# Twenty-four transposes of the identity between the first transposes of x and the first weight unit

## The reference, cut to what matters

```
h = rms_norm(x, g_mix)          # x: 256 x 2048
proj = h @ w_in                 # the first columns computed are those of f
q, k, v, z, f, scal, gates = split(proj)
```

## Time and profile before

| | us |
|---|---|
| median of three runs | 2469.17 |
| the three runs | 2468.76, 2469.17, 2470.74 |
| profiled execution, its own time | 2468.13 |
| its span in the trace | 2466.3 |
| TensorE busy | 2437.7 (99%) |
| VectorE busy | 1534.6 (62%) |
| ScalarE busy | 1031.7 (42%) |
| mean DMA rate | 193 GB/s |

### The profile page before, as it was taken

One profiled execution on the slowest core, in us unless ns is written; L12 is line 12 of the kernel. 1 busy time (PEld: TensorE's weight loads), 2 busy tenths in 40 slices (PEclk: granted clock), 3 DMA queues, 4 the chain that ended last, 5 costly groups with the idle time before them and its releaser, 6 DMA issues.

```text
span 2466.3 us, 31871 instructions
## 1 busy us (share of the span) xinstructions
PE 2437.7 (99%) x13450; PEld 1995.1 (81%) x13450; DVE 1534.6 (62%) x1525; ACT 1031.7 (42%) x859; POOL 267.7 (11%) x222
## 2 busy tenths in 40 slices
PE   8999999999999999999999999999999999999997
PEld 7788888878888887887888888887777778888886
DVE  6465466557676445455445467789999965446664
ACT  4453345324334443433443434443434444544332
POOL 0002200210000000000000000045566400000000
PEclk9999999999999999999999999999999999999999
DMA  7343444346754555455555556675555576566653
GB/s 269 114 151 130 144 168 170 118 137 241 262 200 175 182 193 188 172 191 185 188 189 195 187 200 202 223 243 189 190 195 193 191 280 235 173 240 224 256 196 137
DMA packets 84094, 475.72 MB, mean 193 GB/s; under 512 B 8688, under 2 KB 8816, under 8 KB 32368
## 3 DMA queue, kind: packets, MB, share of 16 engines
q1 hardware_dynamic: 83952, 473.64, 54.8%
HBM read 450.54 MB, written 23.07 MB: 192 GB/s over the span
## 4 chain that ended last, share of the span: by engine, by line
PE 97%; DVE 1%; DMA 1%; issue 0%; ACT 0%; SPq 0%; DVEq 0%; ACTq 0%
PE acc L2071 30%; PE acc L2073 29%; PE acc L2072 29%; PE banks L2229 3%; PE banks L2082 2%; PE banks L2285 1%; PE banks L2352 1%; PE banks L2365 1%; PE banks L2182 1%; DMA av<-spilled 0%; PE banks L2405 0%; PE banks L2387 0%; PE banks L2203 0%; DMA c_in<-in_c_im 0%; DMA raw<-in_w 0%
## 5 line engine op out<-in xcount | busy, mean ns | idle before, releaser
L1257 DVE TENSOR_TENSOR w_lo<-raw,w_hi 128x2048 fp32r<-128x2048 f32 x394 | 908.2, 2308 | 560.6 <-ACT w_hi L815 559.6
L815 ACT ACTIVATE w_hi<-raw 128x2048 fp32r<-128x2048 f32 x394 | 751.7, 1914 | 600.7 <-DMA raw<-in_w 600.5
L2071 PE MATMUL acc<-w_hi,a_hi 128*128 128x512 f32 x2112 | 842.3, 399 | 9.5 <-DVE x_rows L1421 3.8
L2072 PE MATMUL acc<-w_lo,a_hi 128*128 128x512 f32 x2112 | 824.6, 390 | 0.0
L2073 PE MATMUL acc<-w_hi,a_lo 128*128 128x512 f32 x2112 | 824.4, 390 | 0.0
L2071 PEld LDWEIGHTS acc<-w_hi,a_hi 128*128 128x128 f32 x2112 | 397.2, 188 | 110.1 <-issue 21.8
L2073 PEld LDWEIGHTS acc<-w_hi,a_lo 128*128 128x128 f32 x2112 | 397.3, 188 | 85.0
L2072 PEld LDWEIGHTS acc<-w_lo,a_hi 128*128 128x128 f32 x2112 | 397.6, 188 | 79.8 <-issue 1.4
L2071 PE MATMUL acc<-w_hi,b_hi 128*128 128x512 f32 x928 | 364.2, 392 | 0.0
L2073 PE MATMUL acc<-w_hi,b_lo 128*128 128x512 f32 x928 | 361.5, 390 | 0.0
L2072 PE MATMUL acc<-w_lo,b_hi 128*128 128x512 f32 x928 | 361.2, 389 | 0.0
(11 more groups left out here) (349 smaller groups left out, 1636.2 us busy)
## 6 DMA issues: line engine op xcount, KB each, us to landing
raw<-in_w SPq DMA_DIRECT2D x395, 1024.0 KB, 4.9
spilled<-stage SPq DMA_DIRECT2D x72, 256.0 KB, 6.0
gate_in<-spilled SPq DMA_DIRECT2D x20, 512.0 KB, 5.9
x_rows<-in_x SPq DMA_DIRECT2D x4, 512.0 KB, 8.4
x_rows<-in_x SPq DMA_DIRECT2D x1, 2048.0 KB, 9.4
mem_rows<-in_mem SPq DMA_DIRECT2D x2, 1024.0 KB, 6.5
spilled<-stage_b SPq DMA_DIRECT2D x8, 256.0 KB, 5.9
out<-y_rows SPq DMA_DIRECT2D x4, 512.0 KB, 2.7
```

Source lines behind the costliest of these rows:

```text
L815: act.activation(w_hi[:, n % HIGH, :], raw[:, n % RAW, :], ACT.Copy)\
L1257: dve.tensor_tensor(w_lo[:, n % RAW, :], raw[:, n % RAW, :], w_hi[:, n % HIGH, :].bitcast(F32), ALU.subtract).then_inc(lo_split, 1)
L2071: pe.matmul(o, hi[:, tk], wh, start=first, stop=False)
L2072: pe.matmul(o, hi[:, tk], wl, start=False, stop=False)
```

## The change

A constant `WARM = 24` is added. On TensorE, behind `x_in(0)` and before the first unit, 24 transposes are issued. Operand and identity are both `ident`, and the four 128-column quarters of bank 3 are written in turn. They wait for nothing of their own, signal nothing, and nothing reads their result; the bank is overwritten by the transposes of x that use it first.

```
@@ -35,6 +35,7 @@
 HIGH = 4
 AHEAD = 2
 EARLY = 2
+WARM = 24
 EPS = 1e-6
@@ -2437,6 +2438,8 @@
             pe.wait_ge(loaded["small"], 16)
             x_in(0)
+            for q in range(WARM):
+                pe.transpose(bank(3)[:, q % 4 * P:(q % 4 + 1) * P], ident, ident)
 
             def slot_work(n):
                 unit(n, 0)
```

## The result

The changed kernel takes 2476.36 us (median of 12 runs, 2475.54 to 2479.7) against 2468.71 us before (12 runs, 2466.81 to 2470.94): 7.7 us slower, ratio 1.0033 with a 95% interval of 1.0025 to 1.0041. The forecast was 2468.4, with a range to 2471.0. The profiled execution of the changed kernel took 2478.95 us with a span of 2477.1.

A forecast was written before the change was run, and what follows sets the result against it. TensorE's instruction stream, 99% busy, was taken as the bound. Of 1.2 us won at the start 0.5 stay: 2468.7 on the median's scale, less 0.3 credited for clock timing, gives 2468.4 us, range 2467.0 to 2471.0.

The forecast's parts named there:

- The cost of the transposes and the clock: At TensorE's start: 24 transposes from 6.59 us raise the clock at 8.7 and end at 10.2; 1.2 us won by piece 1.
- the wait at 11.3: At TensorE's second matmul group: a new wait for the second quarter of `w_lo`, ready at about 11.4 us.
- The rival of cold transposes: At the start: transposes stay 0.214 us apart, first weight matmul at 11.7, loss of 0.7 to 1.5 us; chance 0.42.
- The cap at unit 6: At unit 6: the chain from unit 5's nearly fixed landing, with 0.47 us to spare, leaves 0.5 of 1.2 us won.
- the forecast's -0.5: At unit 6: the net gain expected to remain of the 1.2 us won at the start, between 0.4 and 1.2.
- Behind unit 6 TensorE is again the bound, nothing is given back and nothing grows: From unit 6 to the end: TensorE 99% busy, so the 0.5 us gain stays unchanged.
- The prediction's last sign of being wrong: Late in the span: a difference between the two traces behind 60 us would speak against the forecast; no size given.
- The rival of a start that runs out of instructions: At the start: TensorE uses up its instructions while DMA is full, waiting up to 3.6 us, time 2472.8; chance 0.04.

The follow-up runs named there:

- e2: The changed kernel, 24 transposes kept, with TensorE's loop pinned to slot 0 of a 256-instruction block: 2464.39 us (0.9978).
- e1: The kernel before, no transposes, with TensorE's loop pinned to slot 236 of a 256-instruction block: 2475.33 us (1.0023).
- e6: The changed kernel, 24 transposes kept, with TensorE's loop put back at slot 188, its worked-out place before the change: 2468.63 us (1.0007).
- e5: The kernel before, no transposes, with TensorE's loop pinned to slot 0 of an instruction block: 2462.57 us (0.9981).
- e8: The kernel before, no transposes, with a prefetch hint for the jump back in TensorE's loop: 2461.45 us (0.9976).
- e10: The changed kernel with a prefetch hint for the jump back, its loop left where it is: 2463.66 us (0.9977).
- e9: The changed kernel with 16 added transposes in place of 24, nothing else changed: 2471.14 us (1.0010).
- e4: The changed kernel with 40 added transposes in place of 24: 2464.14 us (0.9976).
- e7: e2 with VectorE's statistics of x in four parts at earlier places instead of one: 2461.17 us (0.9975).
- e12: The kernel before, no transposes, with the loop at slot 0, the prefetch hint and the statistics of x in four parts: 2461.97 us (0.9975).
- e11: The changed kernel, 24 transposes, with the loop at slot 0, the prefetch hint and the statistics of x in four parts: 2460.01 us (0.9968).

## Why the prediction was wrong

*The cost of the transposes and the clock: right.* The costs were read from the earlier trace rows, and the times came out within 0.3 us: first weight matmul at 9.9 (forecast 10.2), the wait at 11.3 (11.4), the transposes of piece 1 at 13.5 (13.6). That it was so near is in part luck. Over the six profiles with 24 transposes these took 3.43 to 4.68 us, so the clock rose at different times, and the first weight matmul began between 9.89 and 11.12. The gain holds in all: the transposes of piece 1 began at 13.1 to 14.0, against 14.1 to 15.1 in the five kernels without any added. The rival of cold transposes, with 0.42, fell, and with it the rule of the Trainium skill ("TensorE: Matmul & The Clock Gate", Part 4) that the full clock does not engage for transposes: 24 of them in 3.43 us cannot all have run 0.214 us apart.

*The cap at unit 6: right in kind, too small.* I took unit 5's landing as nearly fixed near 31.0. ScalarE began `w_hi` of unit 5 at 31.92 in the changed kernel, against 31.00, and between 30.7 and 32.1 over the other twelve, with and without transposes. So it does not follow the earlier issue, but it scatters by more than the 0.47 us that unit 6 had to spare; here the scatter made +0.5 out of the forecast's -0.5. In e2, with the landing at 31.0, unit 6 is 0.4 us early.

*"Behind unit 6 TensorE is again the bound, nothing is given back and nothing grows": this step failed.* I followed the times of the 48 new instructions and not their place in the program. They move everything behind them, the loop among it, to another place in the 16 KB blocks in which instructions arrive. Behind unit 6, 7 us more were lost where the sum had nothing: 6.1 us in two idle times behind the jumps back, and the low clock there. e1 shows that the place alone makes most of the loss (5.8 of 7.7 us), e6 that the transposes without it do not. The prediction's last sign of being wrong, a difference between the traces behind 60 us, was this one.

*The rival of a start that runs out of instructions* had the right resource, with 0.04, at the wrong place: I put it at the start, where the program runs straight on, and not behind the jumps. Its price of 3.6 us for one such wait was near the 3.15 measured; there are two, and behind each the clock is low.

*Reading the waits.* The earlier trace rows named 3.8 us for `x_rows`, twice 1.9. The table names the last semaphore; e2, e5 and e8 remove the wait without touching VectorE. A wait that stands at a loop's start in each iteration but the first would have been the place to ask for the jump.

## What to carry to other kernels

Instructions added ahead of a large loop have a second cost, which no count of their durations shows: the loop lands elsewhere in the instruction blocks, and each jump back may then cost nothing that shows, or 1.9 us of idle TensorE, or 1.9 and 3 more with a low clock behind. Pin the loop's start or give the jump a prefetch hint before measuring anything small ahead of it; here that was worth 5 to 7 us, several times what the warm start could. And follow a gain at the start down to the first chain that hangs on a transfer.

## What the runs showed of the hardware

- The body of 1654 recorded instructions, 7 blocks of 256, was still held when the loop at slot 0 jumped back (0.21 to 0.23 us). In e8 and e10, with the hint, all 8 blocks that the body touches were held (0.23 to 0.26 us, no transfer of instructions in the second and third round of the loop). In all six profiles with slow jumps a further block came 2.3 to 8 us ahead of the first one, and the loop's first block had to come again. That 8 blocks are held and a ninth pushes out the first is worked out from these counts; no run tests it alone.
- Behind a slow jump the second block let TensorE go on 5.0 to 5.3 us after the first matmul, in the changed kernel, e1 and e9, and 2.3 to 2.4 us after its transfer started.
- The clock fell to 1.2 GHz for about 3.4 us near 104 us in six of the thirteen profiles beside the kernel before (e2, e4, e6, e7, e10, e12), each time within 1 us of the end of 2.6 us of matmuls with 8 and 16 columns, in which TensorE is shown 100% busy. At half speed for 3.4 us it costs an estimated 1.7. Five of the six have 24 or more transposes at the start, but e12 has none, and the changed kernel and e11 have 24 and no such stretch; what decides stays open.
